# The gate of the per-layer embedding in a two-layer decoder kernel: four chunks of 256 columns as two pairs of 512, with the first pair's weight parts in another buffer

## The reference

```
for i in range(2):
    mix = token_mixer(x, positions, w_in[i], ...)          # attention and retention, gated
    x   = layer_norm(alpha * x + mix, ln1_g[i], ln1_b[i])
    ple = sigmoid(x @ w_ple_gate[i]) * (p[i] @ w_ple_proj[i])
    x   = layer_norm(alpha * x + conv_ffn(x, ...) + ple, ln2_g[i], ln2_b[i])
```

## Time and profile before

| | us |
|---|---|
| median of 3 runs | 1495.49 (1495.38 to 1496.31) |
| the profiled execution, its own time | 1496.32 |
| its span, first to last instruction | 1494.4 |
| granted TensorE clock, mean | 0.999 of full speed |
| TensorE busy | 1480.9 (99%) |
| VectorE busy | 1005.7 (67%) |
| ScalarE busy | 775.9 (52%) |
| GpSimd busy | 45.1 (3%) |

### The profile page before, as it was taken

The page is one execution under the profiler, slowest core; times in us unless marked ns, Lnnn a source line. Parts: engine busy times, 40 slices in busy tenths (PEclk is TensorE's granted clock), DMA queues, the critical chain, the costliest instruction groups (busy, mean ns, idle before and its releaser), DMA issues.

```text
span 1494.4 us, 20464 instructions
## 1 busy us (share of the span) xinstructions
PE 1480.9 (99%) x8460; PEld 1304.3 (87%) x8460; DVE 1005.7 (67%) x1134; ACT 775.9 (52%) x826; POOL 45.1 (3%) x24
## 2 busy tenths in 40 slices
PE   9999999999999999999999999999999999999998
PEld 8888888888888988888888888888888888888886
DVE  6575665756655688777866656666567556887777
ACT  5454463554644456656544545546446444566562
POOL 0000000000000010000010000000000000100000
PEclk9999999999999999999999999999999999999999
DMA  9644546455556565656555554455545565655561
GB/s 293 197 151 160 168 141 197 142 169 169 170 169 216 168 219 172 205 192 222 169 170 169 170 169 145 166 175 164 164 146 179 177 208 175 207 201 191 172 239 39
DMA packets 231485, 265.81 MB, mean 178 GB/s; under 512 B 4208, under 2 KB 221808, under 8 KB 230768
## 3 DMA queue, kind: packets, MB, share of 16 engines
q1 hardware_dynamic: 231264, 264.57, 53.5%
q10 hardware_dynamic: 144, 0.13, 0.0%
HBM read 263.64 MB, written 1.05 MB: 177 GB/s over the span
## 4 chain that ended last, share of the span: by engine, by line
PE 93%; DVE 4%; DMA 1%; ACT 1%; issue 1%; SPq 0%; DVEq 0%; ACTq 0%
PE bank L1267 39%; PE bank L1272 20%; PE bank L1253 6%; PE bank L1255 6%; PE bank L1254 6%; PE acc L1253 3%; PE acc L1254 3%; PE acc L1255 3%; PE acc L1407 1%; PE acc L1385 1%; DVE w_lo L744 1%; PE acc L1365 1%; PE acc L1405 1%; PE acc L1381 1%; DMA raw<-w_in 1%
## 5 line engine op out<-in xcount | busy, mean ns | idle before, releaser
L744 DVE TENSOR_TENSOR w_lo<-raw,w_hi 128x2048 fp32r<-128x2048 f32 x239 | 547.3, 2290 | 263.6 <-ACT w_hi L398 263.2
L398 ACT ACTIVATE w_hi<-raw 128x2048 fp32r<-128x2048 f32 x242 | 461.9, 1910 | 146.2 <-PE bank L1255 81.3
L1267 PE MATMUL bank<-xT_both,w_hi 128*128 128x512 f32 x2208 | 528.0, 391 | 0.6 <-DVE mid_lo L969 0.6
L1267 PEld LDWEIGHTS bank<-xT_both,w_hi 128*128 128x128 f32 x2208 | 407.3, 188 | 81.2 <-DVE mid_lo L969 0.8
L1272 PEld LDWEIGHTS bank<-xT_both,w_lo 128*128 128x128 f32 x2208 | 283.1, 191 | 10.7
L1272 PE MATMUL bank<-xT_both,w_lo 128*128 128x256 f32 x2208 | 286.4, 283 | 0.0
L1253 PE MATMUL bank<-w_hi,xT_both 128*128 128x256 f32 (+1 forms) x528 | 176.9, 335 | 3.6 <-DVE w_lo L744 1.8
L512 ACT ACTIVATE scratch<-bank 128x512 f32<-128x512 f32 x80 | 47.9, 598 | 246.9 <-PE bank L1272 246.9
L1255 PE MATMUL bank<-w_hi,xT_both 128*128 128x256 f32 (+1 forms) x528 | 175.6, 333 | 0.0
L1254 PE MATMUL bank<-w_lo,xT_both 128*128 128x256 f32 (+1 forms) x528 | 175.5, 332 | 0.0
L1253 PEld LDWEIGHTS bank<-w_hi,xT_both 128*128 128x128 f32 x528 | 101.0, 191 | 14.9 <-issue 4.9
(11 more groups left out here) (158 smaller groups left out, 1313.9 us busy)
## 6 DMA issues: line engine op xcount, KB each, us to landing
raw<-w_in SPq DMA_DIRECT2D x134, 1024.0 KB, 5.0
raw<-w_up SPq DMA_DIRECT2D x44, 1024.0 KB, 5.1
raw<-w_down SPq DMA_DIRECT2D x20, 1024.0 KB, 5.0
raw<-w_ret_proj SPq DMA_DIRECT2D x16, 1024.0 KB, 4.9
raw<-w_attn_proj SPq DMA_DIRECT2D x8, 1024.0 KB, 5.0
raw<-w_out SPq DMA_DIRECT2D x8, 1024.0 KB, 4.9
raw<-w_ple_gate SPq DMA_DIRECT2D x8, 1024.0 KB, 4.9
scratch<-ln_rows SPq DMA_DIRECT2D x4, 1024.0 KB, 7.6
```

Of the source, the lines that this page charges most:

```text
L398: nc.scalar.activation(w_hi[:, s, :], raw[:, s, :], ACT.Copy).then_inc(hi_ready, 1)
L744: nc.vector.tensor_tensor(w_lo[:, s, :], raw[:, s, :], w_hi[:, s, :].bitcast(F32), ALU.subtract).then_inc(lo_ready, 1)
L1267: mm(pair[p][:, m, :], hi[:, o:o + P], src[:, k0 + k, :, :].rearrange("p a t -> p (a t)"), start=first and k == 0, stop=False)
```

## The change

The four gate chunks are multiplied as two pairs. A pair is one matmul of 512 columns where there were two of 256, so it needs both chunks' parts at once and one bank for each token tile: G0 and G1 go to bank 0 (tile 0) and bank 1 (tile 1), G2 and G3 to banks 2 and 3. The sigmoids, products and residuals go by token tile and 512 columns instead of by chunk.

G0's and G1's high and low parts are written to `ret` (`side_hi`, `side_lo`), which is free once the retention products are done; `last_hi` and `last_lo` move to `attn`. ScalarE writes `side_hi` in four copies of 1024 columns (`to_side_hi`), G0's two ahead of the copy for `C_PLE + 1` and G1's two behind it. GpSimd writes `side_lo` in four subtractions of 1024 columns (`to_half_side_lo`): one ahead of the first `rstd`, three between the two. VectorE no longer makes G1's low part; it counts both side chunks into `lo_ready`, one behind the third sum of the layer norm and one behind the rows of tile 1. ScalarE's copies of G3 and of the first two feed-forward chunks stand elsewhere, and the one of chunk `C_MLP + 1` comes behind the last sigmoid. TensorE transposes tile 1 after five of the eight row blocks of the first pair.

```
-        last_hi = ret[:, 0:4, :, :].rearrange("p a b t -> p (a b t)")
-        last_lo = ret[:, 4:8, :, :].rearrange("p a b t -> p (a b t)")
+        last_hi = attn[:, 0:4, :, :].rearrange("p a b t -> p (a b t)")
+        last_lo = attn[:, 4:8, :, :].rearrange("p a b t -> p (a b t)")
+        side_hi = ret[:, 0:8, :, :] ... rearrange("p (u n) -> p u n", u=2)
+        side_lo = ret[:, 8:16, :, :] ... rearrange("p (u n) -> p u n", u=2)
...
+            def to_side_hi(l, L0, R0, u):
+                s = raw_landed(l, R0, C_PLE + 2 + u)
+                act.wait_ge(chunk_done, L0 + C_PLE - 4 + 1 + RING)
+                for h in range(2):
+                    v = slice(h * CE // 2, (h + 1) * CE // 2)
+                    nc.scalar.activation(side_hi[:, u, v], raw[:, s, v], ACT.Copy).then_inc(side_hi_ready, 1)
...
                 to_hi(l, L0, R0, C_PLE)
-                to_hi(l, L0, R0, C_PLE + 1)
-                to_hi(l, L0, R0, C_PLE + 2)
+                to_side_hi(l, L0, R0, 0)
+                to_hi(l, L0, R0, C_PLE + 1, count=3)
+                to_side_hi(l, L0, R0, 1)
...
                 summed(n2, 2)
+                count_side_lo(side_lo_ready, 4 * l + 2)
                 x_low(n2 + 1, 0)
...
-                count_side_lo(2 * l + 1)
-                to_lo(l, L0, C_PLE + 3)
+                count_side_lo(side_lo_ready, 4 * l + 4)
                 x_low(n2 + 1, 1)
...
+            def to_half_side_lo(l, u, h):
+                pool.wait_ge(side_hi_ready, 4 * l + 2 * u + h + 1)
+                s = slot(l, C_PLE + 2 + u)
+                v = slice(h * CE // 2, (h + 1) * CE // 2)
+                nc.gpsimd.tensor_tensor(side_lo[:, u, v], raw[:, s, v], side_hi[:, u, v].bitcast(F32),
                                         ALU.subtract).then_inc(side_lo_ready, 1)
...
-                rstd(n2, 0)
-                to_side_lo(l, L0, C_PLE + 2)
-                rstd(n2, 1)
+                to_half_side_lo(l, 0, 0)
+                rstd(n2, 0)
+                to_half_side_lo(l, 0, 1)
+                to_half_side_lo(l, 1, 0)
+                to_half_side_lo(l, 1, 1)
+                rstd(n2, 1)
...
+                pe.wait_ge(side_lo_ready, 4 * l + 3)
+                side_pair(0, 0, range(4))
+                pe.wait_ge(side_lo_ready, 4 * l + 4)
+                side_pair(0, 0, range(4, 5))
+                transpose_x(2 * l, 1)
+                side_pair(0, 0, range(5, KT))
                 x_tile_ready(2 * l + 1, 1)
+                pe.wait_ge(bank_read[1], l * USES[1] + (U_PLE[1] + 2))
+                side_pair(1, 1)
+                weights_ready(L0, C_PLE + 5)
+                for t in range(TT):
+                    pe.wait_ge(bank_read[2 + t], l * USES[2 + t] + (U_PLE[2 + t] + 2))
+                    two_chunks(l, C_PLE + 4, 2 + t, t)
```

More of the change, by code:

```diff
@@ L264, in tiles_before @@
         def tiles_before(l, j):
-            return 7 + 2 * j if l else max(2 * j - 1, 0)
+            return 9 + 2 * j if l else max(2 * j - 1, 0)
         @block.sync
@@ L391, in value, with raw_landed, to_hi @@
                 return e if isinstance(e, int) else act.snap(e)
-            def to_hi(l, g, r, c):
+            def raw_landed(l, r, c):
                 s = slot(l, c)
                 act.wait_ge(raw_loaded[s], r + 16 * ((c + l * (C_LAYER % RING)) // RING + 1))
-                act.wait_ge(chunk_done, g + c + 1)
-                nc.scalar.activation(w_hi[:, s, :], raw[:, s, :], ACT.Copy).then_inc(hi_ready, 1)
+                return s
+            def to_hi(l, g, r, c, reader=None, count=1):
+                s = raw_landed(l, r, c)
+                act.wait_ge(chunk_done, g + (c - RING if reader is None else reader) + 1 + RING)
+                nc.scalar.activation(w_hi[:, s, :], raw[:, s, :], ACT.Copy).then_inc(hi_ready, count)
+            def to_side_hi(l, L0, R0, u):
[4 more added lines that the diff above has]
+                    nc.scalar.activation(side_hi[:, u, v], raw[:, s, v], ACT.Copy).then_inc(side_hi_ready, 1)
             def copy_out(g, c, b, dst, scale=1.0, func=ACT.Copy):
@@ L627, in _ @@
                                              ACT.Copy).then_inc(bank_read[2 * u + t], 1)
-                    if u == 0:
-                        to_hi(l, L0, R0, C_PLE + 3)
                 x_high(n2 + 1, 1)
                 to_hi(l, L0, R0, C_PLE + 4)
+                to_hi(l, L0, R0, C_PLE + 5, reader=C_PLE - 1)
                 for j in range(NJ):
-                    to_hi(l, L0, R0, C_PLE + 5 + j) if j < 2 else None
+                    if j == 1:
+                        to_hi(l, L0, R0, C_PLE + 6, reader=C_PLE)
                     if j:
                         act.wait_ge(ple_ready, l * NJ + j)
-                    copy_out(L0, C_PLE + 2 + j, j, ple_sig, func=ACT.Sigmoid)
+                    if j % 2 == 0:
+                        act.wait_ge(tile_done, tiles_before(l, NJ) + j // 2 + 1)
+                    else:
+                        act.wait_ge(chunk_done, L0 + C_PLE + 2 + j + 1 + RING)
+                    nc.scalar.activation(ple_sig, bank[j][:, :], ACT.Sigmoid).then_inc(bank_read[j], 1)
                     if j == 2:
@@ L639, in _ @@
                         nc.scalar.activation(last_hi, last_raw, ACT.Copy).then_inc(last_hi_ready, 1)
-                        to_hi(l, L0 + C_MLP, R0 + 16 * C_MLP // RING, 1)
+                to_hi(l, L0 + C_MLP, R0 + 16 * C_MLP // RING, 1)
                 def take_low(g, c, half, n):
@@ L745, in to_lo, with count_side_lo @@
                                         ALU.subtract).then_inc(lo_ready, 1)
-            def count_side_lo(n):
-                dve.wait_ge(side_lo_ready, n)
+            def count_side_lo(ready, n):
+                dve.wait_ge(ready, n)
                 nc.vector.memset(stat[:, 76:77], 0.0).then_inc(lo_ready, 1)
@@ L1104, in _ @@
                           .then_inc(last_lo_ready, 1)
-                        to_lo(l, L0 + C_MLP, 1)
+                to_lo(l, L0 + C_MLP, 1)
                 def up_sum(half, i):
@@ L1296, in token_half, with side_pair @@
                     ins.then_inc(chunk_done, 1)
+            def side_pair(b, t, ks=range(KT)):
+                for k in ks:
+                    ins = split_product(bank[b][:, :].rearrange("p (u n) -> p u n", u=2),
+                                        xT_hi[:, k, t * P:(t + 1) * P], xT_lo[:, k, t * P:(t + 1) * P],
+                                        side_hi[:, :, k * CH:(k + 1) * CH], side_lo[:, :, k * CH:(k + 1) * CH],
+                                        k == 0, k == KT - 1)
+                if t:
+                    ins.then_inc(chunk_done, 2)
+                elif ks[-1] == KT - 1:
+                    ins.then_inc(tile_done, 1)
             def two_chunks(l, c, b, t, ks=range(KT), every_second=False):
```

39 lines of the change are left out of this document (15 added, 24 removed).

## The result

The changed kernel is slower, as predicted, and by about the predicted amount. Its median is 1502.12 us (six runs, 1500.10 to 1503.99), beside 1495.43 for the kernel before on the same chip (six runs, 1495.06 to 1496.31): a ratio of 1.0044, 95% interval 1.0033 to 1.0055, so 6.7 us more where 6.0 were forecast. The profiled execution took 1501.68 us for a span of 1499.9, which is 5.5 more than before.

The account below looks back on a forecast made before the run. TensorE was taken as the bound, fed by VectorE and GpSimd. Per layer 5.8 us lost less 2.8 saved gives 3.0; two layers on 1496.32 make 1502.3, less 0.83 for the median: 1501.5 us, range 1492.5 to 1505.0.

Parts of the forecast that it names:

- product 1: TensorE's second embedding product, which needs L744's output: forecast to end at 545.7 instead of 540.22, 5.5 us late.
- What bounds: TensorE, busy 1480.9 us, with two gaps of 0.66 and 0.77 us waiting for low parts between embedding products and feed-forward.
- TensorE's saving: Gate stage: wider matmuls and two vanished gaps gain 2.98 us, less about 0.19, so 2.79 us per layer.
- The term for the width: Gate on TensorE: 192 matmuls of 256 columns become 96 of 512, 23.04 to 21.87 us, gain 1.17.
- What I priced at nothing: ScalarE's recut copies, SyncE's later loads, the late copy of chunk `C_MLP + 1` and G3's low part: no cost.
- both fine margins: Spare time: some 0.4 us before the second `up`, some 0.3 us for G3's low part before the second pair.
- The lock: GpSimd's SBUF-reading halves block VectorE's two-input instructions, each half for 2.24 us; 5.8 us lost per layer.
- Who gets the turn: GpSimd is let in between two consecutive two-input VectorE instructions, so three halves delay both L794 and L744, 6.4 us in all.
- VectorE keeps its turn: Rival: VectorE runs its five two-input instructions through before GpSimd's second half; gain 1.1 us per layer, 1493.3, chance 0.15.
- The second half asks too late: Rival: GpSimd's second half slips in behind the first L794; 0.85 us lost per layer, 1497.2, chance 0.13.
- side by side: Rival: GpSimd and VectorE read SBUF together, a meeting costing only 0.10 and 0.57 us; 1489.9, chance 0.17.
- the halves do not shrink: Rival: GpSimd's halves of 1024 columns take longer than 2.24 us; 1504 to 1515, chance 0.05.

Follow-up runs that it names:

- e1: Changed kernel with GpSimd's four half subtractions replaced by memsets that read nothing: 1489.23 us, ratio 0.9958.
- e8: The kernel that splits the low parts between GpSimd and VectorE, with three of four pair groups as 256-column matmuls again: 1493.73 us, ratio 0.9983.
- e2: Changed kernel with GpSimd's last three halves waiting until VectorE's L764 is through: 1493.37 us, ratio 0.9982.
- e3: Changed kernel with GpSimd's four subtractions of 1024 columns cut into eight of 512: 1495.08 us, ratio 0.9997.
- e6: Changed kernel with GpSimd's four halves as a multiplication by 0, one SBUF input instead of two: 1491.15 us, ratio 0.9968.
- e7: Changed kernel with GpSimd's second half waiting for the first half of tile 0's rows: 1493.07 us, ratio 0.9981.
- e10: Changed kernel with GpSimd's second half waiting for tile 0's first rows, plus a tiny GpSimd memset between wait and half: 1493.48 us, ratio 0.9983.
- e9: Changed kernel with GpSimd's second half waiting for VectorE's second row piece (L807) of tile 0: 1496.85 us, ratio 1.0006.
- e11: Changed kernel with GpSimd's third half waiting for the first residual addition (L814) of tile 0: 1496.67 us, ratio 1.0004.
- e4: Changed kernel with eight dummy matmuls on TensorE ahead of each half of tile 0's transposes: 1500.69 us, ratio 1.0032.
- e5: Changed kernel with low parts moved off VectorE's two-input stretch, VectorE doing half of G1, tile 1 transposed after four row blocks: 1490.65 us, ratio 0.9965.

## Why the prediction was right

The times of layer 0, less the 0.26 by which all of it began late:

| step | forecast | measured |
|---|---|---|
| second, third, fourth half end | 535.13, 537.92, 540.71 | 535.11, 537.87, 540.65 |
| L764 ends | 542.81 | 542.80 |
| product 1 ends | 545.7 | 545.86 |
| tile 1's transposes end | 550.35 | 550.19 |
| feed-forward part starts | 569.0 | 568.67 |

- **What bounds.** Right: TensorE, through two places where it waits for VectorE's rows and one low part.
- **TensorE's saving.** A little small: 3.12 and 3.13 per layer in e1's trace, where 2.79 were computed. In the kernel after, the 81 matmuls behind tile 1's transposes took 568.93 - 550.45 = 18.48, which is 81 x 0.228: nothing was lost there of the 0.19 per layer that I had allowed, without a working, for slower first matmuls and the switch. The loss that stands against it was right: the kernel after took 568.93 - 531.74 = 37.19 for the same way, 5.78 more than e1, where 5.8 were forecast. The term for the width, 1.17 for 192 matmuls, agrees with e8: 0.31 per product of 48, four products per layer, 1.24.
- **What I priced at nothing** cost nothing. No wait at the second `up`, none ahead of the second pair, so both fine margins held.
- **The lock.** The decisive step, and right in its sign, size and number: three holds of 2.1 to 2.2 against 2.24. e1 shows that it is the reading, e2 that it is the moment, e3 that the hold scales with the piece. The Trainium skill, page "SBUF — State Buffer", section "Who interferes with whom", says that a VectorE instruction with two SBUF inputs contends with a GpSimd instruction that reads SBUF and not with one that only writes it. The runs agree: 2.85 for one L814 beside the subtraction, 0.74 for the first L814 and 2.28 for L764 beside e1's memsets. What the prediction cited, that the lock is kept for the whole instruction, holds for the subtraction but for its last 0.19 us (each L814 ended 0.55 behind a half and needs 0.74); by e6 a one-input instruction of 2.89 gives it back after some 0.8.
- **Who gets the turn.** Right for this kernel, for a reason that is narrower than I wrote. The root did get in between two L787 (e6 shows it), but from that one change I concluded that GpSimd is let in at each. e7 and e10 show a change at which it isn't. So that all three holds came is in part luck of the start: had the first request come about a microsecond later, as in e7, the rival "VectorE keeps its turn" would have described the chain, and its time, 1493.3, is that of e7. The same section says that issue order decides who blocks. By the starts in the trace, e9 and e11 agree with it and e7 doesn't: GpSimd's start there lay 0.50 ahead of L764's, and it stood back.
- **"The second half asks too late"**, priced at 1497.2, is what e9 built: it measured 1496.85.
- **The missing term.** The clock behind the two gaps. By e4 it adds some 1.4 us to the median, with intervals that overlap, and the 0.33 per layer by which the table's last row was forecast too late make up for half of it. Without the slow stretch the change costs 5.0, with it 6.7; the forecast of 6.0 lies between. That it comes so near to 6.7 is luck, two misses with opposite signs. I had the gaps in the forecast and didn't ask what TensorE does behind them.
- **Of the rivals**, "side by side" is refuted by the first row of VectorE, and "the halves do not shrink" by the halves of 2.5 to 2.8.

## What to carry to other kernels

Before work is moved to GpSimd, list what VectorE runs beside it: each instruction with two SBUF inputs can lose a turn as long as GpSimd's reading, so GpSimd's work belongs beside VectorE's PSUM-input and statistics instructions, which e2's halves left at 0.68 and 0.69, if need be behind an added wait (e2 took back some 9 us). If no such stretch is long enough, VectorE itself is the cheaper place for a part of it (e5: 1.22 us for 1024 columns, against a hold of 2.1 to 2.2). And where a change opens gaps on TensorE, the matmuls behind them have to be priced too, at the slower clock.

## What the runs showed of the hardware

- The granted clock fell to 0.50, the 1.2 GHz level, after TensorE had been busy for 0.65 of 4.7 us, and was 1.00 again some 3 us later. Four transposes between the two waits didn't keep it up; 16 matmuls on zeros did (e4). In e9 and e11 a single wait of 2.1 us was followed by some 3 us at 0.51 in one layer and by none in the other.
- GpSimd's subtraction undisturbed: 2.40 us for 1024 columns (e2), against 4.62 for 2048, so, as an estimate from the two, about 2.17 ns per column and 0.18 fixed.
- With one input, 1024 columns take GpSimd longer (2.77 us undisturbed) than with two (2.40), and yet hold VectorE for 0.78 instead of 2.1 (e6).
- Writing 1024 columns by a memset takes GpSimd 0.95 us, and VectorE's L814 and L764 beside it keep 0.74 and 2.28 (e1).
